# First four GLU groups over quarters of the contraction, with the setup loads issued ahead of them, in an eight-core encoder layer

## What is computed

```
proj = x @ w_in                  # glu_in (2*512) | q | k | v | q_mem | gate_logits
a, g = split(glu_in);  u = a * sigmoid(g)
u = depthwise_conv(u, 31 taps, 'same'); u = silu(layer_norm(u));  y_conv = u @ w_conv_out
s = q k^T / 8 + bias[t5_bucket(k-q)], |k-q| <= 128;  p = softmax([s, sink]);  y_attn = (p v) @ w_attn_out
y_mem = softmax(q_mem (mem w_k)^T) (mem w_v) @ w_mem_out
x = LN(alpha*x + (sum_b sigmoid(gate_b) * y_b) @ w_o)
x = LN(alpha*x + (silu(x w1_gate) * (x w1_up)) @ w2)
```

## Time and profile before

| what | value |
|---|---|
| time before, median of 3 runs | 1064.12 us (1063.47 to 1065.79) |
| span of the profiled execution, slowest core (7) | 1059.0 us |
| spans of the 8 cores | 1045.4 to 1059.0 us |
| PE busy, core 7 | 1000.8 us (95%) |
| DMA moved | 118.38 MB, mean 112 GB/s |

### The profile page before, as it was taken

How to read it: one execution, slowest core, us unless ns; L and a number is a source line. 1 busy time by engine, 2 the same in 40 slices (tenths; PEclk the granted TensorE clock), 3 DMA queues, 4 the chain that set the end, 5 groups by cost and what they waited for, 6 DMA issues and landing times.

```text
span 1059.0 us, 15830 instructions; the slowest of 8 cores (1045.4 to 1059.0 us)
## 1 busy us (share of the span) xinstructions
PE 1000.8 (95%) x5782; PEld 466.9 (44%) x5782; DVE 411.5 (39%) x777; ACT 360.9 (34%) x524; POOL 138.2 (13%) x181
## 2 busy tenths in 40 slices
PE   3999599999999999999998999999999999999996
PEld 1455254544443444444444444444444444444442
DVE  0324166657772222222267544251214321341224
ACT  0135357556652222222235785121111211121111
POOL 3300000212134334333400110000000000000000
PEclk9999799999999999999999999999999999999998
DMA  9899523480019999500291675225431445134301
GB/s 133 152 174 144 116 58 104 84 154 13 17 27 128 160 181 151 101 1 2 61 267 80 161 192 170 90 78 177 155 104 57 157 148 157 40 122 157 120 21 60
DMA packets 40972, 118.38 MB, mean 112 GB/s; under 512 B 5120, under 2 KB 17032, under 8 KB 39648
## 3 DMA queue, kind: packets, MB, share of 16 engines
q0 software_dynamic: 13408, 49.55, 28.0%
q1 hardware_dynamic: 27488, 67.81, 20.7%
HBM read 147.17 MB, written 22.08 MB: 160 GB/s over the span
## 4 chain that ended last, share of the span: by engine, by line
PE 81%; DMA 5%; issue 4%; ACT 4%; DVE 3%; another core or an unknown queue 1%; POOL 1%; DVEq 0%; SPq 0%; ACTq 0%; POOLq 0%
PE ps L231 80%; DMA arena<-xt 2%; DMA arena<-w_out 2%; DVE arena L1018 1%; ACT L1107 1%; ACT L1010 1%; DMA arena<-u_scratch 1%; POOL arena L146 1%; ACT arena L642 0%; ACT arena L1107 0%; ACT mvt L1010 0%; DVE arena L1039 0%; PE ps L685 0%; ACT arena L594 0%
## 5 line engine op out<-in xcount | busy, mean ns | idle before, releaser
L231 PE MATMUL ps<-arena 128*128 128x512 bf16 (+5 forms) x5372 | 984.4, 363 | 41.9 <-DMA arena<-xt 16.6
L231 PEld LDWEIGHTS ps<-arena 128*128 128x128 bf16 (+2 forms) x5372 | 446.7, 98 | 562.8 <-issue 85.8
L1109 DVE TENSOR_TENSOR arena<-ps,arena 128x512 bf16<-128x512 f32 x88 | 59.8, 690 | 192.1 <-PE ps L231 179.3
L826 DVE SCALAR_TENSOR_TENSOR arena<-arena,ps 128x512 f32<-128x512 f32 x96 | 65.9, 686 | 151.8 <-PE ps L231 147.8
L805 ACT ACTIVATE arena<-ps,bgate_sb 128x512 f32<-128x512 f32 x96 | 65.8, 687 | 166.3 <-PE ps L231 166.3
L1107 ACT ACTIVATE arena<-ps 128x512 f32<-128x512 f32 x88 | 51.4, 597 | 180.3 <-PE ps L231 180.2
L997 ACT ACTIVATE arena<-arena 128x1024 bf16<-128x1024 f32 (+1 forms) x32 | 33.7, 1052 | 136.1 <-DVE arena L1130 128.7
L146 POOL DMA_DIRECT2D out<-arena x16 | 8.5, 532 | 408.5 <-DVE arena L1020 408.5
L833 POOL TENSOR_TENSOR arena<-arena 128x512 f32<-128x512 f32 x32 | 40.8, 1275 | 143.6 <-DVE arena L826 143.6
L642 ACT ACTIVATE arena<-ps 128x1024 bf16<-128x1024 f32 x46 | 46.6, 1025 | 12.5 <-PE ps L231 12.3
L838 POOL TENSOR_TENSOR arena<-arena 128x512 bf16<-128x512 f32 x32 | 41.4, 1293 | 45.4 <-DVE arena L826 43.9
(11 more groups left out here) (91 smaller groups left out, 349.6 us busy)
## 6 DMA issues: line engine op xcount, KB each, us to landing
arena<-w_bf_cache SPq DMA_DIRECT2D x88, 512.0 KB, 3.5
arena<-u_scratch SPq DMA_DIRECT2D x64, 135.0 KB, 3.1
arena<-x SPq DMA_DIRECT2D x16, 512.0 KB, 27.9
out<-arena POOLq DMA_DIRECT2D x16, 512.0 KB, 2.9
arena<-w_f POOLq DMA_DIRECT2D x22, 256.0 KB, 6.3
arena<-w_g POOLq DMA_DIRECT2D x9, 512.0 KB, 15.7
arena<-xt POOLq DMA_DIRECT2D x8, 512.0 KB, 34.6
w_bf_cache<-w_f POOLq DMA_DIRECT2D x8, 512.0 KB, 66.5
```

The costliest lines, as they stand in the source:

```text
L231: return pe.run(lambda: nc.tensor.matmul(out, lhsT, rhs, start=start, stop=stop), deps, inc)
L826: t_y = dve.run(lambda: nc.vector.scalar_tensor_tensor(out=gb[r], in0=gb[r], scalar=1.0, in1=ps[:, bk, :], op0=ALU.add, op1=ALU.mult), [tk ...
L1109: t_a = dve.run(lambda: nc.vector.tensor_tensor(out=actT[:, j, :], in0=ps[:, bU, :], in1=sgf[sr], op=ALU.mult), [tU, t_s, e_state["dep"]])
```

## The change

The GLU weights of channels 0 to 255 (c = 0 and 1, both halves) and chunk 0 of x now come as four pairs of 256-KB parts, each for two kc slices. `g_first` gives the four groups of chunk 0 (gate and a, c = 0 and 1) a bank each and does two matmuls of every group as each pair lands. `warm(18)` puts 18 matmuls on zeros ahead of them; its operand is set by a DVE memset. Chunk 1 of x comes in four parts. The loads of w_q, w_kv, w_qm, the memory, w_mkv and chunks 2 and 3 of x are now issued at the start, before POOL's constants. `setup_bias` comes after four groups and not after two. Its load of `Brev` is now issued by SP.

```diff
--- before.py
+++ after.py
@@ -267,6 +267,9 @@
     geb = V(149, [8, 512])
     Brev = V(155.75, [128, 8, 384])
 
+    wz = th2[0].bitcast(BF16)[:, 0:512]
+    t_wz = dve.run(lambda: nc.vector.memset(wz, 0.0))
+
     s_bias, s_small = new_slot("bias"), new_slot("small")
     dma(sp, rb33[:], rbp_d, s_bias)
     t_rb = dma(sp, oh, onehot_d, s_bias)
@@ -279,23 +282,36 @@
     def load(out, in_, deps=(), e=None, name="ld"):
         return dma(e or pool, out, in_, new_slot(name), deps)
 
-    t_glu, t_xt = {}, [[None] * 2 for _ in range(4)]
-
-    def load_glu(c, half=None):
-        for i in ((1, 0) if half is None else (half,)):
+    t_glu, t_xt = {}, [[None] * 4 for _ in range(4)]
+    t_glq = []
+
+    def load_glu(c):
+        for i in (1, 0):
             t_glu[c, i] = load(wglu[:, c, i], w_glu_d[:, c, i])
 
-    def load_xt(k):
-        for h in range(2):
-            t_xt[k][h] = load(xT[:, k, 4 * h:4 * h + 4, :], xt_d[:, k, 4 * h:4 * h + 4, :])
-
-    load_glu(0, 1)
-    load_xt(0)
-    load_glu(0, 0)
-    load_glu(1)
-    load_xt(1)
+    def load_xt(k, n=2):
+        w = 8 // n
+        for h in range(n):
+            t = load(xT[:, k, w * h:w * h + w, :], xt_d[:, k, w * h:w * h + w, :])
+            for q in range(w // 2):
+                t_xt[k][h * w // 2 + q] = t
+
+    for q in range(4):
+        t_glq.append(load(wglu[:, 0:2, :, 2 * q:2 * q + 2, :], w_glu_d[:, 0:2, :, 2 * q:2 * q + 2, :]))
+        t_xt[0][q] = load(xT[:, 0, 2 * q:2 * q + 2, :], xt_d[:, 0, 2 * q:2 * q + 2, :])
+    for c in range(2):
+        for i in range(2):
+            t_glu[c, i] = t_glq
+    load_xt(1, 4)
     load_glu(2)
     load_glu(3)
+    t_wq = load(wq, w_q_d)
+    t_wkv = load(wkv, w_kv_d)
+    t_wqm = load(wqm, w_qm_d)
+    t_memt = load(memT, memt_d)
+    t_wmk = [load(wmk[:, i], w_mkv_d[:, i]) for i in range(2)]
+    load_xt(2)
+    load_xt(3)
 
     t_idz = pool.run(lambda: nc.gpsimd.memset(ident_f[:], 0.0))
     t_identf = pool.run(lambda: nc.gpsimd.affine_select(
@@ -353,7 +369,7 @@
         b, dd = banks.alloc(1)
         for kc in range(8):
             tk = mm(ps[:, b, :], lhs(kc), rhs(kc), kc == 0, kc == 7,
-                    [dd, deps, t_xt[k][0]] if kc == 0 else [t_xt[k][kc // 4]], inc=(kc == 7))
+                    [dd, deps, t_xt[k][0]] if kc == 0 else [t_xt[k][kc // 2]], inc=(kc == 7))
         return b, tk
 
     t_u, t_q, t_k, t_v, t_qm = {}, {}, {}, {}, {}
@@ -361,8 +377,8 @@
     gst = {"i": 0}
     gpend = {}
 
-    def g_gate(k, c):
-        b, tk = group8(lambda kc: wglu[:, c, 1, kc, :], lambda kc: xT[:, k, kc, :], k, [t_glu[c, 1]])
+    def g_gate(k, c, got=None):
+        b, tk = got or group8(lambda kc: wglu[:, c, 1, kc, :], lambda kc: xT[:, k, kc, :], k, [t_glu[c, 1]])
         r = gst["i"] % 3
         gst["i"] += 1
         assert th_free[r] is not None
@@ -371,8 +387,8 @@
         banks.release(b, t)
         gpend[k, c] = (r, t)
 
-    def g_a(k, c):
-        b, tk = group8(lambda kc: wglu[:, c, 0, kc, :], lambda kc: xT[:, k, kc, :], k, [t_glu[c, 0]])
+    def g_a(k, c, got=None):
+        b, tk = got or group8(lambda kc: wglu[:, c, 0, kc, :], lambda kc: xT[:, k, kc, :], k, [t_glu[c, 0]])
         r, t = gpend.pop((k, c))
         t_u[k, c] = dve.run(lambda: nc.vector.scalar_tensor_tensor(
             out=U0[:, c, 32 + k * 512:32 + (k + 1) * 512], in0=th2[r], scalar=1.0, in1=ps[:, b, :],
@@ -381,6 +397,26 @@
         th_free[r] = [t_u[k, c]]
         u_store(k, c)
         uq_pump()
+
+    def warm(n):
+        b, dd = banks.alloc(1)
+        for i in range(n):
+            tk = mm(ps[:, b, :], wz[:, 0:128], wz, True, True, [t_wz] if i == 0 else (), inc=(i == n - 1))
+        banks.release(b, tk)
+        th_free[0] = [tk]
+
+    def g_first():
+        units = [(c, i) for c in range(2) for i in (1, 0)]
+        got = {u: banks.alloc(1) for u in units}
+        for q in range(4):
+            for c, i in units:
+                b, dd = got[c, i]
+                for kc in (2 * q, 2 * q + 1):
+                    tk = mm(ps[:, b, :], wglu[:, c, i, kc, :], xT[:, 0, kc, :], kc == 0, kc == 7,
+                            [dd, t_glq[q], t_xt[0][q]] if kc % 2 == 0 else (), inc=(kc == 7))
+                if q == 3:
+                    (g_gate if i else g_a)(0, c, (b, tk))
+                    tick()
 
     def p_q(k, h):
         b, tk = group8(lambda kc: wq[:, kc, h * 128:(h + 1) * 128], lambda kc: xT[:, k, kc, :], k, [t_wq])
@@ -450,7 +486,7 @@
         banks.release(b, t_b0)
         t_b1 = dve.run(lambda: nc.vector.tensor_tensor(out=geb, in0=ge, in1=rv, op=ALU.mult), [t_b0, t_small])
         btab["st"] = load(gexp_d.ap(), geb, [t_b1], sp)
-        btab["rev"] = load(Brev, bass.AP(gexp_d, 0, [[1, 128], [512, 8], [1, 384]]), [btab["st"]])
+        btab["rev"] = load(Brev, bass.AP(gexp_d, 0, [[1, 128], [512, 8], [1, 384]]), [btab["st"]], sp)
 
     def setup_cw():
         id4b = bass.AP(ident4, 0, [[ident4[:].ap[0][0], 128], [0, 32], [1, 32]])
@@ -884,17 +920,10 @@
     M = [m_steps(u) for u in range(17)]
     CV = [conv_steps(k) for k in range(4)]
 
-    straight(g_list(0, [0]))
+    warm(18)
+    g_first()
     setup_bias()
-    t_wq = load(wq, w_q_d)
-    t_wkv = load(wkv, w_kv_d)
-    t_wqm = load(wqm, w_qm_d)
-    t_memt = load(memT, memt_d)
-    t_wmk = [load(wmk[:, i], w_mkv_d[:, i]) for i in range(2)]
-    load_xt(2)
-    load_xt(3)
-
-    straight(g_list(0, [1]) + [run(setup_cw)] + g_list(1, [0, 1]) +
+    straight([run(setup_cw)] + g_list(1, [0, 1]) +
           g_list(0, [2]) + g_list(1, [2]) + g_list(0, [3]) + g_list(1, [3]))
     for i in range(3):
         uq_load(i)
```

## The result

The changed kernel took 1080.87 us in the median of 4 runs (1076.8 to 1083.84), the kernel before 1063.8 beside it (1060.39 to 1065.79). The ratio is 1.0158, 95% interval 1.0128 to 1.0188: slower by 1.6%, 17 us. I had forecast +2.7 us and a range that ended at 1073. The place where PE is held and the engine that holds it were right, the size was not.

What follows compares the result with a forecast made beforehand. PE was taken as bound by transfers at the start and at 111 us. The start's 0.4 us gain is lost; the late table moves P from 123.4 to 126.1, +2.7 us, giving 1066.8 us, range 1059 to 1073.

Steps and rivals of the forecast that it cites:

- P: Time when PE passes the point at the convolution's second unit, now 123.40 us; forecast 126.1, +2.7 us.
- DVE holds PE near 66: DVE's bias-table copies delay the evacuation of p_v(0); PE stops at 66.3 us and resumes at 80.9.
- the wait at 111: PE's 12.0 us wait for the convolution's second unit, from 111.43 to 123.40 us; forecast gone or under 2 us.
- The count of 1040 packets: Bias table on SP: 1024 runs plus 16 completions, each packet behind one of POOL's.
- Start: ... the load moves from about 40: Bias table on SP: store at about 29.5, 7.1 plus 2 us to land, 1.5 to start the load.
- the bound of 86 on the landing: Latest landing of the bias table, with slow engines as unequal as at the start; likeliest 79 us.
- The length, 38.9 us: Bias table's load on SP: 345 packets until 60 us, the other 695 at 28.7 in a us.
- rival B: Small parts at the start delay everything behind by 3 us; table at 84 to 86, 1072 to 1074; chance 0.10.
- My 0: Cost taken for the GLU weights' 1-KB runs at the start, bounds -1 to +3 us.
- POOL's backlog ends 4.8 us earlier: With the hole in POOL's queue filled, its backlog ends near 112.7 us instead of 117.5; bounds 2 to 8.
- From P to the end I take the kernel as unchanged: Everything behind P, now at 123.40 us, is assumed to take as long as before.
- rival A: Table comes cheaply on SP, DVE waits for nothing, P is 118.6, time 1059.3; chance 0.18.

Runs made afterwards that it cites:

- A: The changed kernel with all parts of the change, against the kernel before; 1080.87 us, ratio 1.0158.
- e1: B with one edit, the load of the bias table issued by SP; 1065.84 us, ratio 1.0035 to B.
- e2: A with the bias table loaded by SP in 128 runs of 7936 bytes instead of 1024 of 768; 1068.94 us, ratio 1.0069 to B.
- e4: B with the new start alone, loads of w_q to chunk 3 behind setup_bias and table on POOL; 1064.23 us, ratio 1.0026 to B.
- B: The kernel before the change, the base of every ratio; 1063.8 us beside the changed kernel.
- e5: A with the six FFN copies issued only when the bias table has landed; 1066.86 us, ratio 1.0059 to B.
- e8: B with the FFN copies issued only after the loads of the convolution's first three units have landed; 1060.03 us, ratio 0.9979 to B.
- e10: B with the early FFN copies in 2-KB rows; 1057.59 us, ratio 0.9953 to B.
- e12: B with its old start, the table in 128 long runs on SP and early FFN copies in 2-KB rows; 1058.82 us, ratio 0.9980 to B.
- e7: A with setup_bias, including table store and load, ahead of the four groups; 1068.37 us, ratio 1.0066 to B.

## Why the prediction was wrong

- That P decides (17.0 of the 19.0 us between the slowest cores lie ahead of the mark), that the table's load is the deciding term, that DVE holds PE near 66, and that the wait at 111 goes: all seen, the last two on every core of A.
- The count of 1040 packets, one for one with POOL's: right. It is one run a packet on SP (0.77 KB, core 0), and not the 9 to 17 descriptors that the Trainium skill (DMA: Bandwidth & Descriptors, "Queues, rings and completion order") gives as typical for a packet. e1 and e2 show that the count decides.
- The failing step is "Start: ... the load moves from about 40", with the bound of 86 on the landing. The store's landing had been put at 7.1 us plus 2 for a second store of u in front. It was 10 to 15.6 us. With the same start but without w_q in POOL's queue it was 4.9 to 7.8 (e4), so what held the store is the loads from w_q on beside it (packets of 6.5 KB on average on core 7 at 38 to 40 us), which never stood there in B; I applied my own rule of one for one to the table and not to its store. The load was then issued at 42.7 to 45.1 on four cores (36.6 to 41.1 on the others), where my sum has it at 38.6. The 1.5 us from issue to first packets were too little as well: about 4 on cores 0, 2, 3, 5 and 7. Together the load moved from 46.5 to 48.5 on the late cores 2, 3 and 7, and from about 41 on cores 0 and 5.
- The length, 38.9 us, was right where nothing came between: about 38 on core 0, from 41 to 78.7.
- The second half of the same step: from there on I let SP's queue run on at 28.7 packets in a us to the end. I had the row for the FFN copies, used it for u's loads only, and did not see that a table 4 us later runs into them. On three of those four cores the table landed at 91 to 97 for it and not by 84, and in time it is the difference between the ratios 1.0059 (e5, copies held back) and 1.0158. On core 3, issued at 42.74, the copies are at 83.3; on core 7, issued 0.7 us later, at 91.3. It was a cliff behind my likeliest value, and my bound of 86 was drawn as if the slope went on.
- "The parts are slow", rival B: partly. PE works steadily 0.9 us later on core 7 (31.64) and 4.2 and 4.4 us later on cores 1 and 2 (31.59 and 30.55, from 27.35 and 26.11); e4 gives +0.26% with all its effects. My 0 rested on the wrong neighbour, the bias table, whose runs are gathered.
- POOL's backlog ends 4.8 us earlier: core 7 of A still has 0.16 MB in 110 to 115 and none after, B has 0.39 MB in 115 to 120. Right. That it would help was wrong: in e2 the wait for u is longer, 15.5 to 19.3 us, and stands one unit earlier.
- "From P to the end I take the kernel as unchanged": this holds for a later P (924 to 933 us behind the mark in A and e5, as in B) and not for an earlier one (932 to 947 in e8). In the forecast only rival A has a much earlier P, and its 1059.3 leans on this assumption.
- The start won nothing that lasts, and the matmuls on zeros nothing that these runs can tell: right.

What stays open: why some cores, and not the same ones in each run, get their four groups 2 to 4 us later than others; why a load of SP moves its first packets only some 4 us after its issue; and where all of the time that e10 wins ahead of the mark goes behind it. No run was made on these.

## What to carry over

When two DMA queues have work, count packets and not bytes: in these runs an urgent load of many short runs on SP moved one run for each packet of POOL's queue, whatever that packet's size. Before a load is moved ahead of others or to another queue, ask which large packets will then stand beside it, at its start and at its latest end, and treat their beginning as an edge and not as a slope. Filling a hole in the DMA queue with bulk work brings the bulk forward, too, and what shares the engines with it pays (e2; e12 against e10 points the same way). And time won early is worth only what the next load lets through (e8: 16.9 us won at the mark on core 7, about 2 in the time).

## What the runs showed of the hardware that was not expected

- Runs of 1 KB in HBM, cast to 512 bytes, with gaps between the runs on both sides, went in packets of 0.75 KB on average in POOL's queue (644 packets for 0.48 MB, core 2 of A, with x's 2-KB runs among them), while runs of 768 bytes that are contiguous at their destination go in packets of 4.7 KB.
- A copy between two HBM tensors with rows of 32 KB moves in packets of 17 KB on average (69 packets for 1.15 MB, core 2 of A), and holds the other queue to 6.7 to 7.5 packets in a us; with rows of 2 KB it is 57 (e10), for about 7 us more of copying.
- The load of the table on SP moved its first packets some 4 us after its issue (e7: issued at 25.49; 13 packets of SP in 25 to 30 us, 302 in the next five; A, core 2: issued at 44.32, none before 48.5). It is not the number of runs: in e2, with 128 runs, it is issued at 41.64 and moves nothing before 45.5.
